# Neighbourhood attention's bias rows, rotary embedding and mask: another layout in DRAM and another place in the program

## The chip, the cores and the metric

One core of a Trainium2 chip runs the whole program: TensorE (PE, with its weight loads as PEld), VectorE (DVE), ScalarE (ACT), GpSimd (POOL), SyncE (SP) and 16 DMA engines. The metric is the device time of one execution in microseconds (us); the median of three runs is compared.

## The reference

Two blocks follow each other. The first has two layers, each made of a feed-forward part, a token mixer and a second feed-forward part; the second block has four layers and isn't touched. The change lies in the token mixer of the first block, which runs once in each of its two layers. Cut to what matters:

```python
def axial_rope(x, rows):                     # on q and k of the 256 tokens of x, 8 heads of 64
    ...
    def rot(xa, pos):
        x1, x2 = jnp.split(xa, 2, axis=-1)
        return jnp.concatenate([x1 * cos - x2 * sin, x2 * cos + x1 * sin], axis=-1)

def neighbourhood_attention(q, k, v, kc, vc, rpb, rows):   # rows = 4 grid rows of 64 tokens
    dr = row_idx - r[:, None]
    dc = np.clip(j[None, :] - j[:, None] + NA_KW - 1, 0, 2 * NA_KW - 2)
    bias = rpb[:, dr + NA_KH - 1][..., dc]
    s_loc = einsum(q, k_blk) * scale
    s_loc = jnp.where(col_valid[:, None, :], s_loc + bias, NEG_INF)
    s_ctx = einsum(q, kc) * scale
    p = softmax(concat(s_loc, s_ctx))
    return p_loc @ v_blk + p_ctx @ vc

def token_mix(hx, hc, w_in, w_out, rpb, w_pool, pool_scale, with_ctx_out):
    qx, kx, vx, ux = split(hx @ w_in)        # the context's hc @ w_in too
    qx, kx = axial_rope(qx), axial_rope(kx)
    na_x = neighbourhood_attention(...)
    pool_x = pool_mix(ux, w_pool, pool_scale)          # windowed means of u
    out_x = concat(na_x, pool_x) @ w_out
```

The bias of query column j and key column c depends on c - j and on the distance of their grid rows alone; a key outside the query's 16 columns is masked.

## The kernel before

Each engine's program is written out by one function, `walk`, which runs over the same text once for each engine and emits what `pe`, `act`, `dve`, `pool` or `sp` guard; counting semaphores tie the engines together. So the order on an engine is the order of the text, and no scheduler changes it.

**Weights.** A product streams its weight matrix in slots of 256 columns and all 1024 rows. `load` (SP) brings a slot into one of 4 buffers `w_raw`; `cut` splits it, half by half, into a high part on ACT (`w_hi`, line 422) and the rest on DVE (`w_lo`, line 425), two slots ahead of PE. PE then runs three matmuls per tile (lines 433 to 435). SP loads the next slot into a buffer when `w_lo` of its old slot is written.

**The mixer** (`mix`). After the norm, POOL waits for everything that was given out before (`border`), and then issues on its DMA queue (`side_load`, line 1079) seven tables (cosines, sines, the matrix `na_swap` that swaps the halves of a rotary pair, the matrix `na_flip`, the mask, two tables of the pooling), `w_pool`, and 16 loads of the bias: for each of 4 query rows and 4 key rows, 64 partitions by 8 heads by 64 columns. Their source is `rpb_pad` in DRAM, which holds the 15 rows of each head's table, each padded to 127 entries. The source's partition pitch is 1 entry, so that partition p gets the row of query column 63 - p: the query columns land in reverse order. `side_wait` waits until every side load issued so far has landed.

PE meanwhile runs `gemm` for q, k and u (2 slot pairs of columns each; ACT evicts them, line 708), each with 512 tokens in the first layer; in the second layer, which needs no context output, q and u have 256 tokens. Then `token_major` makes v, two slots of 4 tiles; with 4 tiles its first slot uses banks 4 to 7 and its second 0 to 3, and DVE copies the tiles out (line 745) behind the cuts of the slot two ahead. POOL runs `pool_windows`, the windowed sums of u, from u's eviction on; only `pool_products`, behind the attention, reads them.

Then two steps stand between v and the attention. First the flip: 8 matmuls of `na_flip` with 512 columns of the bias (line 1290), each turning the query columns round, and behind each on DVE an add of the mask that writes the bias back (line 1295), on two banks in turn. Next `rope_na`: for each of 8 tiles of q and k a matmul with `na_swap` (line 1187), and on DVE a product with the cosines (1189), a product of the swapped tile with the sines (1191) and their sum (1193); the matmul of a tile waits for the sum two tiles before. `border` ahead of it makes PE, ACT and DVE wait for each other. After that `attention` starts: scores on PE (988), bias add and maximum on DVE (1024, 1026), exponentials on ACT (1050), scaling on DVE (1035), transposes on PE (1004), and so on, unit by unit; its first DVE instruction is the bias add of unit 0. In the first layer a second attention, of the context's own queries, follows.

`gemm` takes a generator `between`, which it steps once after each slot pair's work; `token_major` likewise after each slot.

## Time and profile before

| | us |
|---|---|
| median of three runs | 3387.26 |
| lowest and highest of them | 3385.67, 3396.62 |
| the profiled execution's own time | 3391.18 |
| its span, first to last instruction | 3389.5 |

In the span PE is busy for 3127.4 us, DVE for 1704.7, ACT for 1378.5 and POOL for 196.9. The chain that ended last runs almost wholly on PE's products. The mean granted TensorE clock is 0.951 of full speed. The first layer's mixer stands at about 494 to 690 us of the span, the second layer's at about 1580 to 1750. The table is read so: the program is one stream of products on PE, and time is lost where PE stands idle or works on small steps that wait for DVE; two such places lie between the v product and the attention, once in each layer.

### The profile page before, as it was taken

Reading aid. Unit: us, or ns where it says so; the run is one execution under the profiler, and the core shown is the slowest. Engines: PE = TensorE matmul, PEld = TensorE weight load, DVE = VectorE, ACT = ScalarE, POOL = GpSimd, SP = SyncE. Lnnn points to the kernel's source line nnn. Section 1 sums busy time; section 2 is a strip of 40 time slices with the busy share of each in tenths; the row PEclk is TensorE's granted clock in tenths of the full one; section 3 lists DMA queues with packets and bytes.
Section 4 is the critical chain, followed back from the end, with each engine's and each line's share of the span. In section 5 each row is a group of like instructions: output and inputs, shape, how many; then the busy total and the mean of one; then the engine's idle time right before and its main releaser. Section 6 shows DMA issues by size and latency. Waiting matters only on the chain. (4 is left out here: it accounts for less than half of the span.)

```text
span 3389.5 us, 54017 instructions
## 1 busy us (share of the span) xinstructions
PE 3127.4 (92%) x21980; PEld 2738.3 (81%) x21980; DVE 1704.7 (50%) x2636; ACT 1378.5 (41%) x2238; POOL 196.9 (6%) x292
## 2 busy tenths in 40 slices
PE   6999989789999899997889989997799999988998
PEld 4877857467787688876679888997599999988998
DVE  3332262643322533226555547655576677555765
ACT  3222242432222333224255445545364546444654
POOL 1111014001111000001200000000000000000000
PEclk8999989989999899998889999998799999999999
DMA  7555334025554223343325533553155455543453
GB/s 253 174 170 164 100 112 128 1 92 163 168 174 162 87 87 99 99 137 104 87 80 194 187 124 110 193 183 120 38 163 195 156 174 174 187 149 125 150 191 107
DMA packets 403824, 471.35 MB, mean 139 GB/s; under 512 B 9660, under 2 KB 381964, under 8 KB 403626
## 3 DMA queue, kind: packets, MB, share of 16 engines
q1 hardware_dynamic: 380176, 389.05, 35.5%
q0 software_dynamic: 22592, 79.20, 7.5%
q8 instruction: 146, 2.39, 0.3%
q10 hardware_dynamic: 858, 0.29, 0.0%
q14 instruction: 52, 0.43, 0.0%
HBM read 467.33 MB, written 1.20 MB: 138 GB/s over the span
## 5 line engine op out<-in xcount | busy, mean ns | idle before, releaser
L425 DVE TENSOR_TENSOR w_lo<-w_raw,w_hi 128x1024 fp32r<-128x1024 f32 x734 | 896.8, 1227 | 1315.8 <-ACT w_hi L422 1314.8
L433 PE MATMUL bank<-a_hi,w_hi 128*128 128x256 f32 (+1 forms) x3864 | 1242.2, 321 | 69.2 <-DVE a_lo L1352 16.4
L434 PE MATMUL bank<-a_lo,w_hi 128*128 128x256 f32 (+1 forms) x3864 | 1228.6, 318 | 0.0
L435 PE MATMUL bank<-a_hi,w_lo 128*128 128x256 f32 (+1 forms) x3864 | 1226.5, 317 | 0.0
L422 ACT ACTIVATE w_hi<-w_raw 128x1024 fp32r<-128x1024 f32 x734 | 771.2, 1056 | 1012.9 <-PE bank L435 993.9
L433 PEld LDWEIGHTS bank<-a_hi,w_hi 128*128 128x128 f32 x3864 | 743.3, 192 | 147.4 <-issue 81.1
L435 PEld LDWEIGHTS bank<-a_hi,w_lo 128*128 128x128 f32 x3864 | 741.7, 192 | 50.6
L434 PEld LDWEIGHTS bank<-a_lo,w_hi 128*128 128x128 f32 x3864 | 743.3, 192 | 47.7
L433 PE MATMUL bank<-h_hi,w_hi 128*128 128x256 f32 (+1 forms) x1728 | 544.3, 315 | 0.0
L434 PE MATMUL bank<-h_lo,w_hi 128*128 128x256 f32 (+1 forms) x1728 | 539.7, 312 | 0.0
L435 PE MATMUL bank<-h_hi,w_lo 128*128 128x256 f32 (+1 forms) x1728 | 539.2, 312 | 0.0
L433 PEld LDWEIGHTS bank<-h_hi,w_hi 128*128 128x128 f32 x1728 | 326.3, 189 | 30.4 <-issue 9.0
L435 PEld LDWEIGHTS bank<-h_hi,w_lo 128*128 128x128 f32 x1728 | 324.4, 188 | 21.2
L434 PEld LDWEIGHTS bank<-h_lo,w_hi 128*128 128x128 f32 x1728 | 324.4, 188 | 20.0
L487 POOL DMA_DIRECT2D m_raw<-in_w_mod x128 | 95.9, 753 | 1222.5 <-PE bank L498 1040.5
L622 ACT ACTIVATE h_hi<-tmp_y 128x256 f32 (+3 forms) x216 | 94.9, 478 | 76.7 <-DVE tmp_y L675 76.2
L626 DVE TENSOR_TENSOR h_lo<-tmp_y,h_hi 128x256 f32 (+3 forms) x216 | 99.4, 502 | 11.1 <-ACT h_hi L622 9.5
L756 PE MATMUL bank<-tmp_g,ones 128*32 128x64 f32 (+1 forms) x1040 | 53.1, 293 | 54.0 <-ACT tmp_g L776 51.1
L1636 ACT ACTIVATE tmp_g<-bank 128x256 f32<-128x256 f32 x128 | 49.1, 383 | 127.0 <-PE bank L435 126.7
L433 PE MATMUL bank<-w_hi,a_hi 128*128 128x256 f32 (+1 forms) x288 | 82.8, 288 | 10.6 <-DVE v_g L745 10.6
L696 ACT ACTIVATE z<-bank 128x512 f32<-128x512 f32 (+1 forms) x48 | 25.3, 526 | 158.9 <-PE bank L435 158.9
L756 PEld LDWEIGHTS bank<-tmp_g,ones 128*32 128x32 f32 x1040 | 22.2, 118 | 83.1 <-ACT tmp_g L776 71.9
(289 smaller groups left out, 2447.6 us busy)
## 6 DMA issues: line engine op xcount, KB each, us to landing
w_raw<-in_mlp_w SPq DMA_DIRECT2D x128, 1024.0 KB, 5.4
w_raw<-in_w_ffn_gate_up SPq DMA_DIRECT2D x88, 1024.0 KB, 5.2
m_raw<-in_w_mod POOLq DMA_DIRECT2D x128, 512.0 KB, 4.7
w_raw<-in_w_ffn_down SPq DMA_DIRECT2D x32, 1024.0 KB, 6.2
w_raw<-in_gla_w_in SPq DMA_DIRECT2D x24, 1024.0 KB, 5.3
w_raw<-in_w_in SPq DMA_DIRECT2D x16, 1024.0 KB, 6.1
w_raw<-in_ple_w_gate SPq DMA_DIRECT2D x16, 1024.0 KB, 5.2
w_raw<-in_w_ffn_down SPq DMA_DIRECT2D x16, 768.0 KB, 6.2
```

The costliest lines, as they stand in the source:

```text
L422: e.activation(hi, raw, ACT.Copy).then_inc(S.hi_ready.sem, 1)
L425: e.tensor_tensor(lo, raw, hi.bitcast(F32), ALU.subtract).then_inc(S.lo_ready.sem, 1)
L433: e.matmul(dst, hi, rhs_hi, start=start, stop=False)
L434: e.matmul(dst, hi, rhs_lo, start=False, stop=False)
L435: return e.matmul(dst, lo, rhs_hi, start=False, stop=stop)
L487: e.dma_start(m_raw[:, half, :, :], w[:, k0:k0 + 4, ms * SC:ms * SC + SC] if i is None else w[:, k0:k0 + 4, bass.ds(e.snap(i * (per * SC) ...
L622: e.activation(hidden_at(h_hi_f, p, m, i, per, n), tmp_y[:, m, 0:n], ACT.Copy).then_inc(S.hidden_hi.sem, 1)
L626: e.tensor_tensor(hidden_at(h_lo_f, p, m, i, per, n), tmp_y[:, m, 0:n], hidden_at(h_hi_f, p, m, i, per, n).bitcast(F32), ALU.subtract).the ...
L696: e.activation(dst, b[m][:, 0:n], ACT.Copy).then_inc(S.act_evicted.sem, 1)
L756: mm = e.matmul(dst[32 * g:32 * g + 32, 0:w], ones[:, 0:32], src[:, g * w:g * w + w], start=start, stop=stop)
L1636: e.activation(tmp_g[:, m, 0:T], b[m][:, 0:T], ACT.Relu).then_inc(S.act_evicted.sem, 1)
```

## The change

Four things, in both layers.

1. **Bias rows in DRAM.** A new step `repeat_bias`, at the end of the first feed-forward part ahead of its `post_norm`, makes POOL issue 7 DMAs from DRAM to DRAM. Each writes, for one distance of grid rows, the 127 padded entries of 8 heads 64 times over into `rpb_rows`, at a pitch of 128 entries. The 16 bias loads of `mix` then read with a partition pitch of 127 entries, which steps back one entry per query column: the columns land in the right order. Number and shape of the 16 loads stay.
2. **No flip.** The table `na_flip`, its load, its 8 matmuls and 8 DVE adds are gone. The mask is added by `mask_bias`: 2 DVE instructions of 128x2048, both inputs and the output in SBUF, between the two slots of v.
3. **Rotary embedding inside u.** `rope_na` stands after the first slot pair of u's product. Its 8 matmuls go to banks 4 to 7, two to a bank, and wait for nothing of DVE; DVE waits for pairs of them. Ahead of it PE and DVE wait for all side loads (`side_wait`) and for the eviction of q and k. `token_major` now takes banks 0 to 3 for its first slot and 4 to 7 for its second; the second waits for the rotary sums (`at.roped`).
4. **The border before the attention is gone.** PE waits for the copies of v's first slot alone.

The diff, cut to its core:

```diff
@@ token_major
-                turn = 1 if tb > 2 else 0
...
-                        if s == 1:
+                        if s == 1 and tb == 2:
                             e.wait_ge(S.act_evicted.sem, last[0])
                             e.wait_ge(S.dve_evicted.sem, last[1])
+                        if s == 1 and tb > 2:
+                            e.wait_ge(S.dve.sem, at.roped)
...
                         for t in range(tb):
+                            if s == 0 and tb > 2 and t % 2 == 0:
+                                e.wait_ge(S.act_evicted.sem, last[0] - (0 if t else lag[0]))
...
@@ ffn
+                if f == 0:
+                    repeat_bias(layer)
                 post_norm(layer, 4 * f + 1, 6 * f + 2, n, 0.5)
@@
-            def rope_na():
+            def repeat_bias(layer):
+
+                if pool:
+                    side_wait()
+                per_head = 2 * NA_KH - 1
+                for d in range(2 * ROWS - 1):
+                    first = layer * NA_HEADS * per_head + NA_KH - ROWS + d
+                    side_load(rpb_rows[layer, d, :, :, 0:127],
+                              bass.AP(tensor=rpb_pad, offset=first * 127, ap=[[per_head * 127, NA_HEADS], [0, GRID_W], [1, 127]]))
+
+            def rope_na(qk_done):
 
                 base_p, base_d = S.pe.n, S.dve.n
+                if pe or dve:
+                    side_wait()
+                    e.wait_ge(S.act_evicted.sem, qk_done)
                 for j in range(8):
-                    b = bank[6 + j % 2][:, 0:T]
+                    b = bank[4 + j // 2][:, (j % 2) * T:(j % 2) * T + T]
                     if pe:
-                        if j >= 2:
-                            e.wait_ge(S.dve.sem, base_d + 3 * (j - 1))
                         e.matmul(b, Z["na_swap"][:, :], qk[:, j, 0:T], start=True, stop=True).then_inc(S.pe.sem, 1)
...
+            def mask_bias():
+
+                if dve:
+                    side_wait()
+                    for q in range(2):
+                        rows = bias[:, q, :, :].rearrange("p h (r c) -> p (h r) c", c=GRID_W)
+                        e.tensor_tensor(rows, rows, Z["na_mask"][:, :].unsqueeze(1).to_broadcast([P, NA_HEADS * ROWS, GRID_W]),
+                                        ALU.add).then_inc(S.dve.sem, 1)
...
@@ mix
-                            src = bass.AP(tensor=rpb_pad, offset=(layer * rpb_rows + NA_KH - 1 + kr - qrow) * 127,
-                                          ap=[[1, GRID_W], [(2 * NA_KH - 1) * 127, NA_HEADS], [1, GRID_W]])
+                            first = (layer * (2 * ROWS - 1) + ROWS - 1 + kr - qrow) * NA_HEADS * GRID_W * P + GRID_W - 1
+                            src = bass.AP(tensor=rpb_rows, offset=first,
+                                          ap=[[P - 1, GRID_W], [GRID_W * P, NA_HEADS], [1, GRID_W]])
...
                 gemm(w, [(0, DK)], 2, 2, a_op(n), copy_to(ut[:].rearrange("p a t -> p (a t)"), TT, n), S.act_evicted,
-                     first_col=3 * NA_WIDTH)
+                     first_col=3 * NA_WIDTH, between=rope_na(qk_done))
                 pool_windows(n)
                 fetch_table(ACT.Exp)
-                token_major(w, 2 * NA_WIDTH, 2, TT, lambda t, s: v_na[:, t, s * SC:(s + 1) * SC])
...
-                        e.matmul(b[:, :], Z["na_flip"][:, :], flat[:, c], start=True, stop=True).then_inc(S.pe.sem, 1)
...
-                if not pool:
-                    border(but=S.pool)
-                rope_na()
-                pe_wait_all()
+                values_out = S.dve_evicted.n
+                token_major(w, 2 * NA_WIDTH, 2, TT, lambda t, s: v_na[:, t, s * SC:(s + 1) * SC], mask_bias())
+
+                if pe:
+                    e.wait_ge(S.dve_evicted.sem, values_out + 4)
```

Three places in the new order. First DVE in the first layer's mixer, from the cuts of the q, k and u products to the attention (each row: line, instruction, tiles and size; xN is a run of N). Before:

```order
L425 TENSOR_TENSOR w_lo<-w_raw,w_hi 128x8x128 x14
L745 COPY v_na<-bank 128x256 x4
L425 TENSOR_TENSOR w_lo<-w_raw,w_hi 128x8x128 x2
L745 COPY v_na<-bank 128x256 x4
L1295 TENSOR_TENSOR bias<-bank,na_mask_s 128x512 x8
L1189 TENSOR_TENSOR tmp_g<-qk,na_cos_s 128x256
L1191 TENSOR_TENSOR tmp_y<-bank,na_sin_s 128x256
L1193 TENSOR_TENSOR qk<-tmp_g,tmp_y 128x256
...
L1024 TENSOR_TENSOR bank<-bank,bias 128x2x256
```

After (the lines have moved: 423 is 425 before, 1203 to 1207 are 1189 to 1193, 746 is 745, 1027 is 1024):

```order
L423 TENSOR_TENSOR w_lo<-w_raw,w_hi 128x8x128 x10
L1203 TENSOR_TENSOR tmp_g<-qk,na_cos_s 128x256
L1205 TENSOR_TENSOR tmp_y<-bank,na_sin_s 128x256
L1207 TENSOR_TENSOR qk<-tmp_g,tmp_y 128x256
...
L423 TENSOR_TENSOR w_lo<-w_raw,w_hi 128x8x128 x4
L746 COPY v_na<-bank 128x256 x4
L1219 TENSOR_TENSOR bias<-bias,na_mask_s 128x2048 x2
L423 TENSOR_TENSOR w_lo<-w_raw,w_hi 128x8x128 x2
L746 COPY v_na<-bank 128x256 x4
L1027 TENSOR_TENSOR bank<-bank,bias 128x2x256
```

The 24 rotary instructions (eight times the three rows) moved ahead of four cuts and of v's copies, the mask's eight adds became two between v's slots, and the last copies of v stand right ahead of the first bias add.

Second PE in the same layer. Before, behind the last matmul of v:

```order
L435 MATMUL bank<-w_hi,a_lo 128x256
L1290 MATMUL bank<-bias,na_flip_s 128x512 x8
L1187 MATMUL bank<-qk,na_swap_s 128x256 x8
L988 MATMUL bank<-qk 128x512 x6
L1004 MATMUL bank<-eye,prob 128x128 x8
```

After, in the middle of u's product (431 to 433 are the lines of the products):

```order
L432 MATMUL bank<-a_lo,w_hi 128x512
L433 MATMUL bank<-a_hi,w_lo 128x512
L1201 MATMUL bank<-qk,na_swap_s 128x256 x8
L431 MATMUL bank<-a_hi,w_hi 128x512
L432 MATMUL bank<-a_lo,w_hi 128x512
```

The flip is gone, the eight swaps stand between u's first and second slot pair, and the scores follow v's last matmul.

Third POOL's queue from the first layer's last loads of modulation weights (`m_raw`) to the pooling. After (before, the second row wasn't there, `na_flip_s` was loaded behind `na_swap_s`, and the bias came from `rpb_pad`):

```order
L485 DMA m_raw<-in_w_mod 128x4x256 x24
L1082 DMA rpb_rows<-rpb_pad 512x1x127 x7
L1082 DMA na_cos_s<-table_na_cos 128x256
L1082 DMA na_sin_s<-table_na_sin 128x256
L1082 DMA na_swap_s<-table_na_swap 128x128
...
L1082 DMA w_pool_s<-in_w_pool 128x4x128
L1082 DMA bias<-rpb_rows 64x8x64 x16
L1242 MEMSET pool_a 128x320
```

Seven DMAs came in ahead of the tables, and one table left the queue. The second layer has the same three changes.

## Rows read from the trace of the kernel before

**Rows 1.** The table of stretches, first layer: stretch, its length, busy times, PEclk, DMA.

```profile
core 0: us, PE busy (x) PEld busy (x) DVE busy (x) ACT busy (x) POOL busy (x), PEclk, DMA share, GB/s
582.30:588.10 5.80, 0.00 (x0) 0.01 (x1) 4.50 (x6) 2.00 (x2) 5.34 (x7) 0.75 0.04 8
588.10:598.40 10.30, 9.48 (x16) 3.28 (x16) 5.53 (x8) 0.00 (x0) 9.17 (x16) 0.81 0.30 99
598.40:608.10 9.70, 5.30 (x16) 2.46 (x16) 9.39 (x24) 0.00 (x0) 0.71 (x1) 1.00 0.00 0
```

**Rows 2.** The same table, second layer: behind the v product, flip.

```profile
1651.00:1655.90 4.90, 0.00 (x0) 0.00 (x0) 3.69 (x6) 2.00 (x2) 0.00 (x0) 0.77 0.04 9
1655.90:1666.40 10.50, 9.68 (x16) 3.36 (x16) 5.51 (x8) 0.00 (x0) 0.00 (x0) 0.78 0.29 97
```

**Rows 3.** Instructions in order of time, first layer: start, us, engine, line, [idle before <-releaser].

```profile
583.47 3.17 DVE L425 TENSOR_TENSOR w_lo<-w_raw,w_hi 128x1024 fp32r<-128x1024 f32 x2 [7.33 <-ACT w_hi L422]
586.57 1.41 DVE L745 COPY v_na<-bank 128x256 f32<-128x256 f32 x4
...
609.35 0.70 DVE L1024 TENSOR_TENSOR bank<-bank,bias 128x512 f32<-128x512 f32 x1 [1.25 <-PE bank L988]
```

**Rows 4.** The same view, DVE, second layer.

```profile
1652.17 2.36 DVE L425 TENSOR_TENSOR w_lo<-w_raw,w_hi 128x1024 fp32r<-128x1024 f32 x2 [7.28 <-ACT w_hi L422]
1654.45 1.41 DVE L745 COPY v_na<-bank 128x256 f32<-128x256 f32 x4
1678.20 0.70 DVE L1024 TENSOR_TENSOR bank<-bank,bias 128x512 f32<-128x512 f32 x1 [2.18 <-PE bank L988]
```

**Rows 5.** The same view, PE, first layer: the rotary swaps, two records to a matmul.

```profile
598.43 1.10 PE L1187 MATMUL bank<-qk,na_swap_s 128*128 128x256 f32 x4 [0.83 <-issue]
600.24 0.70 PE L1187 MATMUL bank<-qk,na_swap_s 128*128 128x256 f32 x2 [0.71 <-DVE qk L1193]
```

**Rows 6.** The same view, POOL: issues of the bias loads in both layers.

```profile
506.81 2.76 POOL L1079 DMA_DIRECT2D bias<-rpb_pad  x4
...
529.35 3.39 POOL L1079 DMA_DIRECT2D bias<-rpb_pad  x5 [6.96 <-issue]
...
1593.87 2.76 POOL L1079 DMA_DIRECT2D bias<-rpb_pad  x4
...
1617.57 3.39 POOL L1079 DMA_DIRECT2D bias<-rpb_pad  x5 [7.42 <-issue]
```

**Rows 7.** The bias tile: landing times of the last five (first layer), last two (second).

```profile
DMA to landing us min/median/max: 4.9/7.1/7.2
...
DMA to landing us min/median/max: 7.1/7.3/7.5
```

**Rows 8.** Instructions in order of time, ACT: last eviction of u's first pair, both layers.

```profile
548.41 0.60 ACT L708 ACTIVATE ut<-bank 128x512 f32<-128x512 f32 x1 [3.89 <-PE bank L435]
...
1622.23 0.38 ACT L708 ACTIVATE ut<-bank 128x256 f32<-128x256 f32 x1 [1.55 <-PE bank L435]
```

**Rows 9.** The same view, DVE, first layer, during the u and v products.

```profile
549.99 1.23 DVE L425 TENSOR_TENSOR w_lo<-w_raw,w_hi 128x1024 fp32r<-128x1024 f32 x1 [4.21 <-ACT w_hi L422]
555.43 1.23 DVE L425 TENSOR_TENSOR w_lo<-w_raw,w_hi 128x1024 fp32r<-128x1024 f32 x1 [4.21 <-ACT w_hi L422]
...
574.74 1.40 DVE L745 COPY v_na<-bank 128x256 f32<-128x256 f32 x4
```

**Rows 10.** The qk tile, all its cosine products: min/median/max ns.

```profile
L1189 DVE TENSOR_TENSOR tmp_g<-qk,na_cos_s x16: 417/419/969, 598.4 to 1674.8; 128x256 f32<-128x256 f32 x16
```

**Rows 11.** Instructions in order of time, POOL: a pooling step, and the idle time before the tables.

```profile
502.33 0.55 POOL L1079 DMA_DIRECT2D na_cos_s<-table_na_cos  x1 [55.31 <-issue]
...
598.39 0.73 POOL L1225 TENSOR_TENSOR ut<-pool_b,ut 128x256 f32<-128x256 f32 x1
...
1589.40 0.55 POOL L1079 DMA_DIRECT2D na_cos_s<-table_na_cos  x1 [94.42 <-ACT qk L708]
```

**Rows 12.** DMA queue of POOL, stretch 506 to 560: packets, MB, share of 16 engines.

```profile
q0 software_dynamic: 1050, 3.02, 25.4%
```

More of the change, by code:

```diff
@@ L169, in constants @@
     c["na_cos"], c["na_sin"], c["na_swap"] = cos, sin, swap
-    eye_row = np.eye(GRID_W, dtype=np.float32)[::-1]
-    c["na_flip"] = np.kron(np.eye(P // GRID_W, dtype=np.float32), eye_row)
     col = np.arange(GRID_W)
@@ L270, in build @@
             Z["na_swap"] = sb("na_swap_s", [P, P], F32, h)
-            Z["na_flip"] = sb("na_flip_s", [P, P], F32, h)
             Z["na_mask"] = sb("na_mask_s", [P, GRID_W], F32, h)
@@ L333, in build @@
         rpb_pad = nc.dram_tensor("rpb_pad", [DEPTH, NA_HEADS * (2 * NA_KH - 1), 127], F32)
+        rpb_rows = nc.dram_tensor("rpb_rows", [DEPTH, 2 * ROWS - 1, NA_HEADS, GRID_W, P], F32)
         total, shift_from = [], []
@@ L738, in token_major @@
                                 v_hi, v_lo = (cut_slot(x, nn)[:, k, :] for x in (w_hi, w_lo))
-                                mm = three(bank[(s + turn) % 2 * tb + t][:, 0:SC], x_hi, x_lo, v_hi, v_lo, k == 0, k == DK - 1)
+                                mm = three(bank[s % 2 * tb + t][:, 0:SC], x_hi, x_lo, v_hi, v_lo, k == 0, k == DK - 1)
                         mm.then_inc(S.slot_used.sem, 2)
@@ L744, in token_major @@
                         for t in range(tb):
-                            e.tensor_copy(dst(t, s), bank[(s + turn) % 2 * tb + t][:, 0:SC]).then_inc(S.dve_evicted.sem, 1)
+                            e.tensor_copy(dst(t, s), bank[s % 2 * tb + t][:, 0:SC]).then_inc(S.dve_evicted.sem, 1)
                     S.dve_evicted.n += tb
@@ L1189, in rope_na @@
                         e.tensor_tensor(tmp_g[:, j % 2, 0:T], qk[:, j, 0:T], Z["na_cos"][:, :], ALU.mult).then_inc(S.dve.sem, 1)
-                        e.wait_ge(S.pe.sem, base_p + j + 1)
+                        e.wait_ge(S.pe.sem, base_p + 2 * (j // 2) + 2)
                         e.tensor_tensor(tmp_y[:, j % 2, 0:T], b, Z["na_sin"][:, :], ALU.mult).then_inc(S.dve.sem, 1)
@@ L1195, in rope_na @@
                 S.dve.n += 24
+                at.roped = S.dve.n
+                yield
+            def mask_bias():
[5 more added lines that the diff above has]
+                                        ALU.add).then_inc(S.dve.sem, 1)
+                S.dve.n += 2
+                yield
             def pool_windows(n):
@@ L1256, in mix @@
                     border()
-                for name in ("na_cos", "na_sin", "na_swap", "na_flip", "na_mask", "pool_row", "pool_ctx"):
+                for name in ("na_cos", "na_sin", "na_swap", "na_mask", "pool_row", "pool_ctx"):
                     side_load(Z[name][:], C[name][:])
                 side_load(Z["w_pool"][:, :, :], A["w_pool"][layer].rearrange("g c d -> c g d"))
-                rpb_rows = NA_HEADS * (2 * NA_KH - 1)
                 for qt in range(2):
@@ L1273, in mix @@
                 gemm(w, [(0, DK)], 2, 2, a_op(TT), copy_to(qk_f[:, 4 * TT:], TT, TT), S.act_evicted, first_col=NA_WIDTH)
+                qk_done = S.act_evicted.n
                 gemm(w, [(0, DK)], 2, 2, a_op(n), copy_to(ut[:].rearrange("p a t -> p (a t)"), TT, n), S.act_evicted,
-                     first_col=3 * NA_WIDTH)
+                     first_col=3 * NA_WIDTH, between=rope_na(qk_done))
                 pool_windows(n)
                 fetch_table(ACT.Exp)
-                token_major(w, 2 * NA_WIDTH, 2, TT, lambda t, s: v_na[:, t, s * SC:(s + 1) * SC])
-                flat = bias[:, :, :, :].rearrange("p q h c -> p (q h c)")
-                base_p, base_d = S.pe.n, S.dve.n
-                for j in range(8):
-                    c, b = slice(j * 512, j * 512 + 512), bank[4 + j % 2]
-                    if pe:
-                        if j == 0:
-                            side_wait()
-                            e.wait_ge(S.dve_evicted.sem, S.dve_evicted.n)
-                        if j >= 2:
-                            e.wait_ge(S.dve.sem, base_d + j - 1)
-                        e.matmul(b[:, :], Z["na_flip"][:, :], flat[:, c], start=True, stop=True).then_inc(S.pe.sem, 1)
-                    if dve:
-                        if j == 0:
-                            side_wait()
-                        e.wait_ge(S.pe.sem, base_p + j + 1)
-                        e.tensor_tensor(flat[:, c].rearrange("p (r c) -> p r c", c=GRID_W), b[:, :].rearrange("p (r c) -> p r c", c=GRID_W),
-                                        Z["na_mask"][:, :].unsqueeze(1).to_broadcast([P, 512 // GRID_W, GRID_W]), ALU.add).then_inc(S.dve.sem, 1)
-                S.pe.n += 8
-                S.dve.n += 8
-                if not pool:
-                    border(but=S.pool)
-                rope_na()
-                pe_wait_all()
+                values_out = S.dve_evicted.n
+                token_major(w, 2 * NA_WIDTH, 2, TT, lambda t, s: v_na[:, t, s * SC:(s + 1) * SC], mask_bias())
+                if pe:
+                    e.wait_ge(S.dve_evicted.sem, values_out + 4)
+                if dve:
+                    e.wait_ge(S.dve.sem, S.dve.n)
                 def head_rows(m):
```

## The prediction, made before the changed kernel ran

> **What bounds the kernel now.** I read the table of stretches first, since the change touches two places only, the way from the v product to the attention in each layer. PE's v product ends at 582.3 in the first layer and at 1651.0 in the second. Behind it PE does nothing for 5.8 and 4.9 us, then works at flips for 10.3 and 10.5 us, and in the first layer at the rotary step for 9.7 us, in which DVE is busy for 9.39 us [rows 1, 2]. Next the rows in order of time. What the attention starts with on DVE is its first bias add, at 609.35 and 1678.20 [rows 3, 4]. From there it runs the same units as before, so I take the gain of a layer as the time by which this instruction comes earlier. In each place a chain decides, not an engine's load: DVE's cuts and copies of v, then flips and mask adds in turn, then 24 rotary instructions. Without flip and rotary step, what is late next is DVE, which has two cuts and four copies to do after v: it is free at 586.57 + 1.41 = 587.98 and at 1654.45 + 1.41 = 1655.86 [rows 3, 4].
>
> **What goes.** From DVE's last copy to the bias add: 609.35 - 587.98 = 21.4 us and 1678.20 - 1655.86 = 22.3 us, **43.7 us** in all. Flips, mask adds, rotary step, border and the first score's way (1.25 us and 2.18 us of waiting, rows 3 and 4) all lie in it. The scores of units 0 and 1 now run on PE beside DVE's cuts and copies, since PE waits only for the copies of v's first slot, and their banks (0 to 3) are the ones these copies empty.
>
> **What the swaps cost on PE.** Eight matmuls now stand in the midst of u's product, where PE is fully busy. Two took 1.10 us and one alone 0.70 [rows 5], so each further one adds 0.40: 0.70 + 7 x 0.40 = **3.5 us** a layer, 7.0 in all; at 1.10 a pair it would be 4.4 a layer. Everything behind them is later by that. They wait for nothing of DVE, since each has a half bank of its own.
>
> **What the rotary instructions cost on DVE.** 24 instructions, some 9.7 us [rows 1], go between the cuts. In the first layer the cut ahead of them ends at 549.99 + 1.23 = 551.2, so they end near 561; the cut that stood at 555.43, then due near 558.9, slips to 561 [rows 9]. It feeds v's second slot. DVE copied v's first slot from 574.74 on, behind two cuts [rows 9], so PE wants the second near 571 + 3.5, 13 us later: nothing. The next load of weights slips with it, under a stock of four buffers: nothing. PE's new wait for the last rotary sum stands ahead of that same slot: nothing. If this cover were gone, the cost would be the 2 us by which the cut slips.
>
> **The mask.** Two instructions of 2048 columns, both inputs in SBUF. A cut of 1024 columns takes 1.23 us [rows 9], a product of 256 takes 0.42 [rows 10]: 1.055 ns a column, so 2.3 us each, 4.6 in all. POOL's windows run beside them. What that does, the cuts show: two took 3.17 us where POOL was at work and 1.23 each where it wasn't [rows 1, 3, 9], and one cosine product took 969 ns instead of 419 while POOL's step of 0.73 us began at 598.39 [rows 10, 11]. So up to 6.1 us. They start at 574.74 + 1.40 + 3.5 = 579.6 in the first layer [rows 9] and end by 585.7 at the latest; the next work on DVE comes at 583.47 + 3.5 = 587.0 [rows 3]. Hidden, with 1.3 us to spare at worst.
>
> The Trainium skill says of this (SBUF — State Buffer, Who interferes with whom) that a VectorE instruction with two SBUF inputs shares a read port with GpSimd instructions that read SBUF, one of them blocking the other whole. By that rule the 0.55 us of the cosine product is a full block, and these rows agree.
>
> What isn't hidden: the first layer's attention now starts while POOL's windows still run. They end near 599.1 [rows 11]; with the later u and the mask in their way near 604, and DVE's attention starts at 591.5. Three or four units, each with two scalings in SBUF, could wait up to 0.5 us apiece, 3.5 us at most, nothing at least; I take **1.5 us**. In the second layer the windows end before the attention.
>
> **The new wait for the side loads.** PE and DVE now wait, after u's first slot pair, until all 16 bias loads have landed; before, this wait came after v and never ended last. Queued behind it are PE's swaps, u's second pair and all of v. First layer: the last load's issue ends at 529.35 + 3.39 = 532.7, one issue is 0.69, so it begins at 532.1, and lands 7.2 us later at 539.3 [rows 6, 7]. PE arrives as ACT evicts u's first pair, at 548.4 [rows 8]: nothing, with 9 us to spare. Second layer: q and u have half the tokens, and PE arrives at **1622.2** [rows 8]. The last load begins at 1617.57 + 3.39 - 0.69 = 1620.3 and lands 7.1 to 7.5 us later, at 1627.4 to 1627.8 [rows 6, 7]; without the load of the flip table, one issue of about 0.54 [rows 11], at **1627.1**. So a stall of **5 us**, the one new wait on the path. If POOL's bursts of issues fell otherwise it could be 0 or 8.
>
> A stall brings the clock down: behind the idle 5.8 and 4.9 us the flips had a granted clock of 0.81 and 0.78 [rows 1, 2], which between the levels of 2.4 and 1.2 GHz is 0.38 x 10.3 = 3.9 and 0.44 x 10.5 = 4.6 us at half speed. Half of that is lost: **2 us**. DVE's mask and rotary work come later with PE and stay covered; the cuts of the second half of u come after the rotary sums.
>
> **Repeating the rows.** Seven DMAs a layer of 512 rows of 508 bytes, 260 KB each. They stand in POOL's queue behind the last loads of modulation weights, and ahead of a stretch in which POOL has nothing to do for 55 and 94 us [rows 11]. Issued like the bias loads (a burst, a pause of some 8 us, another), they need about 15 us, and land within 10 more. What they move, 1.8 MB, costs by the rate of POOL's queue: 0.254 x 16 x 54 us over 1050 packets is 0.21 us for 2.9 KB [rows 12], so 1.8 MB is about 8 us of all 16 engines. PE's weights are four slots ahead. Cost nothing; if that cover were gone, up to 8 us a layer. The Trainium skill speaks against this step (DMA: Bandwidth & Descriptors, Specifications): below 512 bytes the transfer isn't at line rate and turns into a read-modify-write. No row here shows a write of 508 bytes; even at three times the price the step would end within POOL's idle time, so the sum stays.
>
> **The sum.** 43.7 gone; 7.0 for swaps, 5 for the stall, 2 for the clock and 1.5 for POOL's windows added: a gain of **28.2 us**. The first layer gives 21.4 - 3.5 - 1.5 = 16.4, the second 22.3 - 3.5 - 7 = 11.8. The profiled execution's own time of 3391.18 would become 3363.0. It lies 3.9 us above the median of the runs, which is what counts: 3387.26 - 28.2 = **3359**.
>
> **The rivals.**
> *No stall in the second layer.* If the loads from the new rows land 5 us sooner, the 7 us of stall and clock stay: gain 35, 3352. For it: three bursts at some 12 us each leave room for one burst fewer, with one table less in the queue [rows 6]. Against it: the number of loads is the same.
> *The bias loads get slower, and it ends slower than before.* A load's 512 pieces of 256 bytes used to come from a few KB that overlap; now they come from 8 blocks 32 KB apart at a pitch of 508 bytes. From first issue to last landing it takes 539.3 - 506.8 = 32.5 us and 1627.6 - 1593.9 = 33.7 us now [rows 6, 7]. Stretched by f, it stalls PE by 32.5 f - 42 in the first layer and by 33.7 f - 29 in the second. Without stalls the change gains 43.7 - 7.0 - 1.5 = 35 us, so it breaks even, with the clock, at f = 1.55. At f = 2 the stalls are 23 and 38 us, with the clock 65: slower by 30, 3417. For it: the wait moved ahead of v, 29 us after the first issue. Against it: pieces, bytes and issues are the same, and the pauses between bursts are POOL's. At f from 1.2 to 1.5 the gain shrinks to between 19 and 4 us.
> *The start isn't what counts.* Could the attention be held by PE or ACT instead of DVE, or the product behind it start no sooner? POOL's windows, near 604, are far from the pooling's products, which stand behind the attention. Then only half would come through: 14 us, 3373. I see no row for it.
>
> **How the numbers follow.** Forecast (28 us, give or take 6) 0.62; no stall 0.14; loads slower by 1.2 to 1.5, or half of it lost, 0.14, of which 0.04 is a gain too small to tell; a stretch near break-even 0.04; slower 0.06. About 0.3%, 10 us, can be told from no change. So faster 0.86, same 0.08, slower 0.06. The range is 3350 to 3374: it takes in the case without a stall, swaps at 4.4, a stall of 8, and a partly stretched load; beyond it lie about 2 in 10.
>
> **What would show it.** In the changed profile: no flip; swaps of 3.5 us between u's pairs in both layers; ahead of them in the second layer a PE idle time of about 5 us ended by a side load, none in the first; two mask instructions of 2.3 to 3 us between v's copies; DVE's first bias add right behind v's last copy, 5 to 6 us after v's end; the repeats on POOL well before the norm's end. It is wrong if the side loads land late in the first layer too, if the mask pushes v's cuts, or if PE stops at the end of the first feed-forward part, where the repeats move data.

## The result, and the profile after

The changed kernel takes **3357.09 us** (median of 4 runs, 3344.98 to 3360.89), the kernel before 3391.85 in 4 runs (3385.67 to 3396.62): a ratio of 0.9892, with a 95% interval of 0.9877 to 0.9907. The profiled execution took 3360.89 us, with a span of 3358.5. Forecast were 3359 us and a gain of 28.2 us; between the medians the gain is **34.8 us**. The number was met more closely than the gain, since the kernel before has a median 4.6 us higher over 4 runs than over the 3 runs that the forecast started from.

The first layer, DVE in order of time (start, us, engine, line, what, idle time before and what ended it):

```profile
550.05 1.22 DVE L423 TENSOR_TENSOR w_lo<-w_raw,w_hi 128x1024 fp32r<-128x1024 f32 x1 [4.21 <-ACT w_hi L420]
551.19 0.42 DVE L1203 TENSOR_TENSOR tmp_g<-qk,na_cos_s 128x256 f32<-128x256 f32 x1
...
559.88 0.43 DVE L1207 TENSOR_TENSOR qk<-tmp_g,tmp_y 128x256 f32<-128x256 f32 x1
560.23 1.22 DVE L423 TENSOR_TENSOR w_lo<-w_raw,w_hi 128x1024 fp32r<-128x1024 f32 x1
...
578.29 1.40 DVE L746 COPY v_na<-bank 128x256 f32<-128x256 f32 x4
579.62 5.03 DVE L1219 TENSOR_TENSOR bias<-bias,na_mask_s 128x2048 f32<-128x2048 f32 x2
587.03 2.94 DVE L423 TENSOR_TENSOR w_lo<-w_raw,w_hi 128x1024 fp32r<-128x1024 f32 x2 [2.39 <-ACT w_hi L420]
589.90 1.40 DVE L746 COPY v_na<-bank 128x256 f32<-128x256 f32 x4
591.23 0.68 DVE L1027 TENSOR_TENSOR bank<-bank,bias 128x512 f32<-128x512 f32 x1
```

The rotary step is done by 560.3, within u's product; the mask stands between v's first copies and its last cuts; and the first bias add follows the last copy with no gap, where [rows 3] had 21.4 us between them. The same in the second layer, to be held against [rows 4]:

```profile
1631.64 5.42 DVE L1219 TENSOR_TENSOR bias<-bias,na_mask_s 128x2048 f32<-128x2048 f32 x2
1638.47 2.89 DVE L423 TENSOR_TENSOR w_lo<-w_raw,w_hi 128x1024 fp32r<-128x1024 f32 x2 [1.41 <-ACT w_hi L420]
1641.29 1.40 DVE L746 COPY v_na<-bank 128x256 f32<-128x256 f32 x4
1642.61 0.68 DVE L1027 TENSOR_TENSOR bank<-bank,bias 128x512 f32<-128x512 f32 x1
```

The same view for ACT, the last eviction of u's first pair, in both layers; then for PE, the swaps at the same places.

```profile
548.48 0.60 ACT L706 ACTIVATE ut<-bank 128x512 f32<-128x512 f32 x1 [3.90 <-PE bank L433]
...
1605.08 0.38 ACT L706 ACTIVATE ut<-bank 128x256 f32<-128x256 f32 x1 [1.55 <-PE bank L433]
```

```profile
548.28 3.62 PE L1201 MATMUL bank<-qk,na_swap_s 128*128 128x256 f32 x16
...
1604.88 3.62 PE L1201 MATMUL bank<-qk,na_swap_s 128*128 128x256 f32 x16
```

Neither row of swaps has idle time before it. The stall forecast for the second layer isn't there. With this eviction as zero, the first bias add stood at 60.94 us before (609.35 - 548.41) and stands at 42.75 now (591.23 - 548.48): 18.2 us gained in the first layer. In the second, 1678.20 - 1622.23 = 55.97 has become 1642.61 - 1605.08 = 37.53: **18.4 us**, where 11.8 were forecast. Together that is 36.6 us. The second layer's first bias add comes 35.6 us earlier; the 1.0 us between lies behind the first layer's first bias add, from which to the second layer's eviction of u it takes 1013.9 us instead of 1012.9.

Why PE didn't wait shows on POOL, where the seven repeats come first and then, in both layers, the issues of the side loads:

```profile
447.05 1.67 POOL L1082 DMA_DIRECT2D rpb_rows<-rpb_pad  x2
450.14 0.79 POOL L1082 DMA_DIRECT2D rpb_rows<-rpb_pad  x1 [1.41 <-issue]
457.58 2.36 POOL L1082 DMA_DIRECT2D rpb_rows<-rpb_pad  x3 [6.66 <-issue]
467.31 0.79 POOL L1082 DMA_DIRECT2D rpb_rows<-rpb_pad  x1 [7.37 <-issue]
502.49 0.58 POOL L1082 DMA_DIRECT2D na_cos_s<-table_na_cos  x1 [34.39 <-issue]
...
506.46 2.10 POOL L1082 DMA_DIRECT2D bias<-rpb_rows  x3
512.99 4.79 POOL L1082 DMA_DIRECT2D bias<-rpb_rows  x7 [4.43 <-issue]
522.19 4.11 POOL L1082 DMA_DIRECT2D bias<-rpb_rows  x6 [4.41 <-issue]
...
1576.28 2.07 POOL L1082 DMA_DIRECT2D bias<-rpb_rows  x3
1586.50 4.83 POOL L1082 DMA_DIRECT2D bias<-rpb_rows  x7 [8.15 <-issue]
1594.85 4.08 POOL L1082 DMA_DIRECT2D bias<-rpb_rows  x6 [3.52 <-issue]
```

Before, the bursts were 4, 7 and 5 loads with pauses of 8.07 and 6.96 us in the first layer and 8.76 and 7.42 in the second. Now they are 3, 7 and 6, with pauses of 4.43 and 4.41, and of 8.15 and 3.52. From the first issue to the end of the last, the loads take 19.8 and 22.7 us, not 25.9 and 27.1 [rows 6], and in the second layer the last lands 3.4 us after its issue instead of 7.1 to 7.5 [rows 7]. That is at 1598.2 + 3.4 = 1601.6, and PE comes at 1604.88.

### The profile page after: what moved, and what is told of

Read it like the earlier page. It is cut to its first block and busy times, and to the rows that moved or that the text cites. A ratio compares the mean times of both kernels' runs of the same rounds, so it can differ in the third digit from the quotient of the medians.

```text
span 3358.5 us, 53925 instructions
## 1 busy us (share of the span) xinstructions
PE 3108.9 (93%) x21948; PEld 2741.9 (82%) x21948; DVE 1706.7 (51%) x2624; ACT 1377.6 (41%) x2238; POOL 216.4 (6%) x304
```

## The experiments

Executions of one kernel scatter by 10 to 20 us, so a difference of a few us is read from the trace, at three places. The last two columns are the program's unchanged rest: from that bias add to the start of the second block (POOL's load of `in_p`), and from there to the end of the span.

| kernel | first bias add, layer 1 | layer 2 | to the second block | to the end |
|---|---|---|---|---|
| before | 609.35 | 1678.20 | 276.0 | 1435.3 |
| after | 591.23 | 1642.61 | 280.4 | 1435.5 |
| after, again | 590.35 | 1641.30 | 282.9 | 1433.9 |
| old source | 589.78 | 1640.67 | 277.6 | 1435.9 |
| rotary step alone | 600.66 | 1670.81 | 279.4 | 1440.4 |
| no flip alone | 604.59 | 1664.88 | 282.5 | 1440.8 |
| no repeats | 591.88 | 1648.73 | 278.5 | 1421.6 |
| table back | 591.65 | 1648.61 | 278.2 | 1433.6 |
| repeats twice | 591.99 | 1644.88 | 278.7 | 1422.8 |
| late cuts | 586.37 | 1634.45 | 277.7 | 1435.2 |
| late cuts, again | 586.92 | 1635.16 | 277.4 | 1440.4 |
| loads made twice | 603.74 | 1683.32 | 285.5 | 1428.8 |
| no windows | 588.89 | 1639.87 | 278.0 | 1436.9 |
| neither flip nor windows | 599.42 | 1657.66 | 277.5 | 1433.6 |

### Does the source set the pace of the loads?

Theory A: reading from the repeated rows makes a load land sooner. Theory B: the new source isn't the cause. The changed kernel, with the loads pointed at the old rows at the old pitch:

```diff
-src = bass.AP(tensor=rpb_rows, offset=first, ap=[[P - 1, GRID_W], [GRID_W * P, NA_HEADS], [1, GRID_W]])
+src = bass.AP(tensor=rpb_pad, offset=(layer * NA_HEADS * (2 * NA_KH - 1) + NA_KH - 1 + kr - qrow) * 127,
+              ap=[[1, GRID_W], [(2 * NA_KH - 1) * 127, NA_HEADS], [1, GRID_W]])
```

> The changed kernel, but its 16 bias loads read the padded table at the old pitch of one entry again (so the bias rows reach the attention with the query columns reversed); the repeats are still made. Question: why did the bias loads take some 25 us instead of 33, so that no stall came in the second layer? Theory A, the source sets the pace (64 partitions reading overlapping bytes are slow): the loads take 32 to 34 us again in both layers, PE waits about 5 us for a side load after u's first pair in the second layer, the time is 5 to 7 us above the changed kernel's (about 3363 against 3357). Theory B, the queue does it (one table fewer, other bursts): the loads stay at 23 to 25 us, no stall, same time as the changed kernel.

Measured: 3357.25 us (4 runs, 3354.30 to 3365.02), a ratio to before of 0.9899 (0.988 to 0.9918). The bursts are 3, 7 and 6 loads, the last landing in the second layer is at about 1600.5, and there is no stall. Theory A falls: where the bytes come from doesn't matter. The rival by which the new pitch slows the loads falls with it.

### The rotary step alone

The kernel before, with the eight swaps and 24 rotary instructions inside u's product; flip and mask adds stay behind v:

```diff
-     first_col=3 * NA_WIDTH)
+     first_col=3 * NA_WIDTH, between=rope_na(qk_done))
...
-rope_na()
```

> The kernel before with only the rotary step moved into u's product (with the banks of v turned round as in the change); flips, mask adds and old bias source stay. Theory: the rotary step's 9.7 and 10 us leave the way to the attention, 3.5 us of swaps a layer come in, and with the old source the second layer stalls 5 us with 2 us of clock: a gain of about 6 us, 3386 against 3392. Rival, no stall even with the old source: a gain of about 13 us, 3379.

Measured: 3391.75 us against 3394.96, a ratio of 0.9993 (0.9979 to 1.0008; 10 runs): nothing that can be told from no change, and too little for the rival's 13 us. In the first layer the bias add is 54.4 us from u's eviction instead of 60.9, a gain of 6.5; in the second it is 58.9 instead of 56.0, a loss of 3.0. There the bursts are 4, 7 and 5 as before, and the stall that the prediction had foreseen appears. PE in order of time:

```profile
1618.49 6.00 PE L1191 MATMUL bank<-qk,na_swap_s 128*128 128x256 f32 x16 [6.65 <-DMA bias<-rpb_pad]
```

The list of waits from 1605 to 1630 (who waited for what: us in all, times, longest):

```profile
PE bank L1191 <- DMA bias<-rpb_pad: 6.7, 1, 6.7
```

The swaps take 6.00 us behind the stall and 3.62 without one: 2.4 us of clock, where the prediction had put 2. So the mechanism exists and was sized nearly right (6.7 and 2.4 against 5 and 2); it is the changed kernel that doesn't meet it.

### The flip gone alone

The changed kernel, with the rotary step back behind v, and its border:

```diff
-     first_col=3 * NA_WIDTH, between=rope_na(qk_done))
+     first_col=3 * NA_WIDTH)
...
+if not pool:
+    border(but=S.pool)
+next(rope_na(qk_done))
+pe_wait_all()
```

> The changed kernel with the rotary step back behind v, with the border ahead of it: only the flip goes, and the mask moves between v's slots. Theory: the flips' 10.3 and 10.5 us go, nothing comes in: a gain of 19 to 22 us against the kernel before, about 3371. Rival, that the border and v's copies hide a part: a gain under 15 us.

Measured: 3380.34 us (5 runs, 3377.68 to 3390.44), a ratio of 0.9958 (0.9944 to 0.9972): 14 us gained, not 21. The table of stretches, from the end of v's last copy to the first bias add, in both layers (stretch, length, busy time and count of PE, PEld, DVE, ACT and POOL, PEclk, DMA share, GB/s):

```profile
587.30:604.60 17.30, 7.71 (x22) 5.44 (x24) 13.19 (x25) 0.00 (x0) 14.11 (x22) 0.70 0.17 59
1651.70:1664.90 13.20, 7.78 (x22) 5.43 (x24) 8.97 (x26) 0.00 (x0) 0.00 (x0) 0.76 0.23 77
```

DVE in order of time, in the first of them:

```profile
590.57 0.94 DVE L1201 TENSOR_TENSOR tmp_g<-qk,na_cos_s 128x256 f32<-128x256 f32 x1
591.44 0.41 DVE L1203 TENSOR_TENSOR tmp_y<-bank,na_sin_s 128x256 f32<-128x256 f32 x1
```

In the first layer the step takes 17.3 us and DVE is busy for 13.2 of them: POOL's windows, which the flips used to cover, now run beside it, and most products with the cosines, whose two inputs lie in SBUF, take 0.85 to 0.96 us instead of 0.42. The product with a bank as input keeps 0.41. In both layers the clock is low, which it had not been behind the flips of the first [rows 1]. The gain lies on the rival's side of 15 us, but not for the rival's reason: ahead of the first rotary instruction, where the border stands, DVE idles for 0.4 us only. That is also all that any run shows of the border's price; none took it away alone.

The same kernel without POOL's windows:

```diff
-pool_windows(n)
```

> The kernel without the flip and with the rotary step still behind v, now also without the pooling's windows. With the windows the rotary step of the first layer took from 587.3 to the bias add at 604.6, 17.3 us, where before the flips it had taken 11.4. Theory, two causes: the windows block the cosine and sum instructions on DVE (about 4 us of the 6), and the swaps start at a low clock since nothing warms PE ahead of them (about 2 us). Without the windows it takes 13 to 13.5 us, as in the second layer. Rival, the clock alone: it stays at 17 us.

Measured: 3370.39 us in one run, and 13.2 us from v's last copy to the bias add in the first layer, against 17.3. So the windows cost 4.1 us there. What is left stands 2.2 us in the first layer and 1.4 in the second above rotary step and first score of before (609.35 - 598.4 = 11.0 and 1678.2 - 1666.4 = 11.8). In both layers of this run the granted clock of the stage is 0.76, and the eight swaps take about 5.8 us where they take 3.62 inside u's product. That the clock is the cause of the rest is likely, but no run separates it from the new order of waits.

By the medians the parts alone give 3 us (not told from nothing) and 14 us, the whole gives 35. By the bias add's distance from u's eviction it is 6.5 - 3.0 = 3.5 us for the rotary step, 4.3 + 9.0 = 13.3 us for the flip, and 36.6 us for the whole. Each part alone leaves work behind v, and puts it where something else costs it: the rotary step moved alone meets the loads, the flip gone alone uncovers windows and clock.

### Why the loads come sooner

Now the question was what makes the bursts differ. Theory C: the repeats ahead in the queue; theory D: the table that is gone. Without the repeats, and with the old source of the loads, which the first experiment shows to change nothing:

```diff
-if f == 0:
-    repeat_bias(layer)
```

> The changed kernel with the old source of the bias loads and without the 14 repeats (the bias rows arrive with the query columns reversed). Question: what made the bias loads quick, since the old source kept them quick. Theory C, the repeats, which stand in POOL's queue ahead of them, leave the queue in another state, so that the bursts of issues fall as 3, 7 and 6: without them the bursts are 4, 7 and 5 or the like again, the loads take 30 to 34 us, PE waits 5 to 7 us for a side load in the second layer, and the time is 7 to 9 us above the changed kernel's (3364 to 3366). Theory D, the missing flip table does it: bursts 3, 7, 6, 23 to 26 us, no stall, 3357.

Measured: 3354.46 us (4 runs, 3350.45 to 3359.58), a ratio of 0.9887 (0.987 to 0.9903). POOL in order of time, second layer, and PE's swaps:

```profile
1576.45 3.43 POOL L1080 DMA_DIRECT2D bias<-rpb_pad  x5
1588.48 4.75 POOL L1080 DMA_DIRECT2D bias<-rpb_pad  x7 [8.60 <-issue]
1600.43 2.72 POOL L1080 DMA_DIRECT2D bias<-rpb_pad  x4 [7.19 <-issue]
...
1609.59 5.41 PE L1199 MATMUL bank<-qk,na_swap_s 128*128 128x256 f32 x16 [4.30 <-DMA bias<-rpb_pad]
```

The stall of 4.3 us is there, and the bias add stands 43.40 us behind u's eviction instead of 37.53. So 5.9 us up to the second layer's attention hang on the repeats being in the queue. The total time doesn't show them: 7 to 9 us above the changed kernel were expected, and the median lies 2.6 below it. In the profiled execution the second block, which the edit doesn't touch, was 14 us faster (the table above); the other three executions have no trace. So whether the 5.9 us reach the end isn't shown.

With the flip's table loaded again, unused:

```diff
-for name in ("na_cos", "na_sin", "na_swap", "na_mask", "pool_row", "pool_ctx"):
+for name in ("na_cos", "na_sin", "na_swap", "na_flip", "na_mask", "pool_row", "pool_ctx"):
```

> The changed kernel with the flip table loaded again, though nothing reads it: an eighth load ahead of the bias loads. Theory C (the repeats decide): the bias loads stay at 23 to 26 us and PE doesn't wait in the second layer. Theory D (the table decides): 32 to 34 us, and a stall of 5 to 7 us there.

Measured: 3362.07 us (one run), with bursts of 2, 7 and 7. Both theories fail. It is fast in the first layer and not in the second, where these rows stand on POOL and PE:

```profile
1587.23 4.76 POOL L1085 DMA_DIRECT2D bias<-rpb_rows  x7 [8.98 <-issue]
1598.50 4.75 POOL L1085 DMA_DIRECT2D bias<-rpb_rows  x7 [6.51 <-issue]
...
1609.47 5.41 PE L1204 MATMUL bank<-qk,na_swap_s 128*128 128x256 f32 x16 [4.41 <-DMA bias<-rpb_rows]
```

With the repeats issued twice:

```diff
-for d in range(2 * ROWS - 1):
+for d in [*range(2 * ROWS - 1)] * 2:
```

> The changed kernel with every repeat made twice, 14 DMAs a layer in place of 7. Theory that their own time is hidden in POOL's idle stretch: the norm behind them starts no later, and PE idles no longer at the end of the first feed-forward part. By theory C the bursts of the bias loads shift once more: first burst other than 3, span of the loads anything from 23 to 34 us; by theory D they stay at 3, 7, 6.

Measured: 3348.01 us (one run), with bursts of 1, 7, 7 and 1, and a stall of 1.57 us in the second layer. The tables' first issue comes at 503.21 instead of 502.49, and at 503.09 without any repeat: 14 repeats still cost the norm nothing. In the second layer the same: from the first layer's bias add to the eviction of u it takes 1013.5 us with 14 repeats and with none.

Neither C nor D alone, then, but **when a burst meets a weight load**. Two rules hold for the side loads in all these traces. The first burst, tables included, is 12 loads without repeats (8 + 4, or 7 + 5), 10 with seven repeats (7 + 3, or 8 + 2) and 8 with fourteen (7 + 1); each later one is 7 or the rest. (The repeats themselves go out three at a time at most.) And a pause ends about 0.4 us after the whole burst ahead of it has landed. Most bias loads land 3 to 5 us after their issue, or 6 to 9 where one of SP's loads of 1 MB is issued during the burst. The second burst of the second layer, beside the issue of SP's weight load next to it:

| kernel | second burst | SP's weight load | longest landing | pause behind | stall |
|---|---|---|---|---|---|
| before | 1605.39 to 1610.16 | 1608.43 | 7.7 | 7.42 | the wait stood behind v |
| rotary step alone | 1596.53 to 1601.31 | 1598.08 | 7.9 | 7.57 | 6.65 |
| old source | 1584.53 to 1589.38 | 1589.34 | 4.2 | 3.85 | 0 |
| repeats twice | 1585.33 to 1590.09 | 1591.69 | 4.0 | 3.63 | 1.57 |
| after | 1586.50 to 1591.33 | 1591.28 | 3.8 | 3.52 | 0 |
| table back | 1587.23 to 1591.99 | 1591.31 | 6.8 | 6.51 | 4.41 |
| no repeats | 1588.48 to 1593.23 | 1591.53 | 7.5 | 7.19 | 4.30 |

The landing times of this burst in the changed kernel, and then in the kernel without repeats:

```profile
DMA to landing us min/median/max: 3.1/3.6/3.8
```

```profile
DMA to landing us min/median/max: 3.0/3.3/7.5
```

The changed kernel's burst ends as the weight load is issued, and with the table back, where it ends 0.7 us later, the pause is 3 us longer. The first layer agrees: before, the second burst stood from 517.64 to 522.39 about a weight load issued at 518.61, and its longest landing was 7.3 us; in the changed kernel it ended at 517.78, ahead of the load at 518.66, and its longest was 4.7. No run moved the weight load alone, so this is read from the traces and not shown by an edit. The stall of "repeats twice" has another cause: its sixteenth load needs a fourth burst. The Trainium skill (DMA: Bandwidth & Descriptors, Queues, rings and completion order) says that each DMA engine takes the queues for which it has work in turn, a packet at a time; the longer landings beside a weight load (7.5 against 3.8 us) agree with it, but no run here shows the turns themselves. What in the queue sets the length of the first burst wasn't tried and stays open.

### Is the new wait on the path at all?

Each bias load issued twice, the second time into a buffer that isn't in use then:

```diff
 side_load(bias[half * GRID_W:(half + 1) * GRID_W, qt, :, kr * GRID_W:(kr + 1) * GRID_W], src)
+other = (prob, probT)[qt][half * GRID_W:(half + 1) * GRID_W, :, :, :].rearrange("p a b (c d) -> p (a b c) d", d=T)
+side_load(other[:, :, kr * GRID_W:(kr + 1) * GRID_W], src)
```

> The changed kernel with each bias load made a second time, into buffers that are free then: 32 loads. It prices the new wait. Theory: the side loads take about 48 us, so PE waits after u's first pair about 4 to 8 us in the first layer and about 20 us in the second, both ended by a side load, and the time is 25 to 35 us above the changed kernel's, near that of the kernel before. Rival, that PE's wait is covered by other slack: under 10 us.

Measured: 3399.3 us (one run), 42 above the changed kernel and 5 above the kernel before. PE's swaps of the first layer:

```profile
558.90 5.47 PE L1201 MATMUL bank<-qk,na_swap_s 128*128 128x256 f32 x16 [9.27 <-DMA probT<-rpb_rows]
```

And of the second:

```profile
1643.90 5.69 PE L1201 MATMUL bank<-qk,na_swap_s 128*128 128x256 f32 x16 [24.30 <-DMA probT<-rpb_rows]
```

Both stalls, 9.3 and 24.3 us, are longer than expected, and so is the loss (42 us, expected 25 to 35). The first bias add of the second layer is 40.7 us later than in the changed kernel. So the wait is on the path in both layers, and the loads' pace decides on which side of zero it falls: the mechanism of the rival that ended slower is real, and only its cause, the pitch, isn't.

### The price of POOL's windows

The changed kernel without them (the rotary step stays where the change puts it):

```diff
-pool_windows(n)
```

> The changed kernel without the pooling's windows on POOL (u goes into the pooling's products as it is). It prices what POOL's windows cost DVE in the first layer. Theory, the shared port: the two mask instructions take 2.3 us each in place of 2.5 to 2.8, the four scalings of the units that ran beside the windows take 0.88 a pair in place of 1.2 to 1.55, and the eighth bias add of the first layer comes 23 us after the first instead of 23.8; 1 to 2 us in all in this stage, too little for the total time to show. Rival, that the slower scalings were covered by waits anyway: the distance from the first to the eighth bias add stays.

Measured: 3357.08 us (one run). A step of the windows beside the mask in the changed kernel, POOL in order of time:

```profile
579.66 2.84 POOL L1252 TENSOR_TENSOR ut<-pool_b,ut 128x256 f32<-128x256 f32 x1
```

The mask and a pair of scalings without the windows, DVE in order of time:

```profile
577.38 4.48 DVE L1219 TENSOR_TENSOR bias<-bias,na_mask_s 128x2048 f32<-128x2048 f32 x2
...
592.81 0.88 DVE L1038 TENSOR_SCALAR prob<-prob,stat 128x512 f32<-128x512 f32 x2
```

The mask takes 4.48 us without the windows and 5.03 beside them, and POOL's step beside it 2.84 instead of 0.73. From first to eighth bias add it is 23.2 us instead of 23.8: the windows cost the attention 0.6 us, with scalings of 1.2 to 1.6 us a pair instead of 0.88. Another 0.6 us lies ahead of it: the first bias add stands 42.16 us behind u's eviction instead of 42.75, since v's last two cuts take 2.36 us instead of 2.94. The kernel before paid that too (3.17 us, [rows 3]). By the Trainium skill (SBUF — State Buffer, Who interferes with whom) the one that comes second is blocked whole; the step on POOL, longer by 2.1 us where one mask instruction takes 2.3, agrees.

### One step further

Now v's last cuts, which serve the output product, stand ahead of the attention on DVE. Made behind `pool_products` instead:

```diff
-ahead(nn, None, 0)
+if s < slots - 1 or tb == 2:
+    ahead(nn, None, 0)
...
 pool_products(layer, n)
+ahead(at.slot - 1, None, 0)
```

> The changed kernel with one more move: the cuts of the second slot of the output product, which stand ahead of v's last copies on DVE, are made after the pooling's products instead. Theory that DVE's work behind v is what the attention waits for: DVE is free 1.4 us after v instead of 5 to 6, then the first score (about 2.9 us after v's end) ends last, so the first bias add comes 2 to 3 us earlier in each layer and the time is about 5 us below the changed kernel's (3352). Rival, that the late cuts are then waited for by the output product, or that POOL's windows hold the attention back: no gain, or 2 to 4 us lost.

Measured: 3355.44 us (4 runs), a ratio of 0.9898 (0.9878 to 0.9918). In the trace, DVE copies v and adds the bias at once:

```profile
585.04 1.42 DVE L747 COPY v_na<-bank 128x256 f32<-128x256 f32 x4 [1.24 <-PE bank L433]
586.37 0.69 DVE L1028 TENSOR_TENSOR bank<-bank,bias 128x512 f32<-128x512 f32 x1
```

To tell, both kernels were run again on one chip.

> The changed kernel with the two cuts behind v made after the pooling's products. In its first profile the first bias add came 3.9 us earlier behind u's eviction in the first layer and 4.0 in the second. Theory, that this is on the path: 3 to 8 us below the changed kernel. Rival, that the late cuts or POOL's windows take it back: no difference.

> The changed kernel once more, beside the next one on the same chip: 1.0 to 1.2 per cent below the kernel before.

Measured: 3353.97 us with late cuts (6 runs, 3340.42 to 3363.89; ratio 0.9886, 0.9867 to 0.9905), and 3359.08 for the changed kernel (5 runs, 3349.82 to 3361.14; ratio 0.9899, 0.9884 to 0.9914). By the trace the bias add comes about 4 us sooner in each layer (38.74 and 33.58 us behind u's eviction, not 42.75 and 37.53), and the second layer's stands at 1634.45 and 1635.16 against 1640.67 to 1642.61. About 1 us of this is lost again on the way to the second layer (1014.5 and 1014.7 us from the first bias add to u's eviction, against 1013.9 and 1013.4). Over both sets of runs the medians are 3354.8 and 3359.1. By the trace the attention starts sooner; between the medians the 4 us aren't told apart from scatter, as the intervals overlap.

## Why the prediction was right, and where it wasn't

The time was met within 2 us and the gain missed by 6.6, and that the first is so close is luck: the 7 us of stall and clock that didn't come were made up for by a start value, 3387.26, that lay 4.6 us below the median over 4 runs. Term by term:

- **What goes, 43.7 us**: right. DVE was what came last, and the bias add follows its last copy with no gap in either layer. From the same eviction on, the first layer gains 18.2 (21.4 - 3.5 = 17.9 worked out), the second 18.4 (22.3 - 3.5 = 18.8).
- **Swaps**: 3.62 us a layer, forecast 3.5. They wait for nothing of DVE.
- **Rotary instructions**: 9.1 us from 551.19 on, forecast 9.7; the slipped cut at 560.23, forecast 561; nothing waits for it.
- **Mask**: 5.03 and 5.42 us, inside the forecast 4.6 to 6.1, and hidden: DVE still idles 2.39 and 1.41 us before v's next cuts.
- **POOL's windows**: 0.6 us, forecast 1.5. They run until 606.9 and not 604; single steps of theirs take up to 2.84 us beside the mask and the cuts.
- **Repeats**: 20 us from first issue to last, forecast 15, and landings of 6.1 to 8.5 in the first layer; the norm's end is where it was (502.49 against 502.33). The Trainium skill's rule against writes below 512 bytes (DMA: Bandwidth & Descriptors, Specifications) wasn't put to the test, as no run repeated rows of 512 bytes; what the runs show is that the repeats, once or twice over, delay nothing that is on the path.
- **The new wait for the side loads, 5 us and 2 for the clock: this step failed.** It took the pace of the loads (three bursts, pauses of 7 and 8 us, landing after 7.1 to 7.5) unchanged from the trace of before, corrected only by one table's issue. The changed kernel's own queue has another rhythm: the repeats shorten the first burst by two loads, and with the flip's table gone as well the second burst ends at 1591.33, just as SP's weight load is issued (1591.28), so that the last load lands 3.3 us before PE comes. Either alone isn't enough: without the repeats PE stalls for 4.30 us, with the table back for 4.41. The rival "no stall" gave the gain as 35 us, but neither of its reasons is what happened: the new rows aren't what makes the loads land sooner, and there are still three bursts. Nearer was the remark that bursts falling otherwise could make the stall 0 or 8.
- **The clock**: no stall, no loss. Where stalls were made, it cost 1.8 to 2.4 us on the swaps, as forecast.
- **The loads get slower**: no; neither pitch nor source matters. Two figures of this rival don't follow from its own formula: at f of 1.2 and 1.5 it leaves a gain of about 22 and 3 us, not 19 and 4. Nothing rests on them.
- **The start isn't what counts**: no. The first bias add of the second layer is 35.6 us earlier. The profiled span is shorter by 31.0 only; the 4.6 lie behind that bias add, in work that is unchanged, and the table of kernels shows that stretch between 276.0 and 285.5 us, with the kernel before at the low end. What goes with it is the granted clock (the third number from the right), here in two stretches of the changed kernel behind the attention:

```profile
1676.00:1724.40 48.40, 36.89 (x326) 32.57 (x325) 23.62 (x45) 22.29 (x42) 0.00 (x0) 0.76 0.27 88
1724.40:1764.40 40.00, 40.00 (x337) 40.00 (x337) 22.93 (x33) 20.55 (x30) 0.00 (x0) 0.95 0.46 150
```

The answering stretches of before have 0.82 and 1.00. Whether this is chance of the execution, or something of the changed kernel, one trace of before can't tell; it stays open.

## What to carry to other kernels

Work between a product and the step that it feeds can move inside the product, if it needs nothing of it. There it costs only its time on the engine that is busy (3.6 us of swaps a layer here), and nothing on those that have room. But take everything out of the gap at once, since each part alone left another obstacle in it (3.5 and 13.3 us alone, 36.6 together). When a wait is moved ahead, its price hangs on the rhythm of a queue that the same change alters: give the stall a range that reaches to nothing, and look what else is in that queue. And read an edit of a few us at a fixed place in the trace, not from the total, where unchanged code scatters by more.

## What the hardware did that I had not expected

- POOL's queue issues bias loads in bursts of seven, and goes on about 0.4 us after the whole burst has landed; 7 or 14 transfers issued long before shorten the burst behind them by 2 or 4 loads.
- One weight load of 1 MB that meets a burst raises its longest landing from 3.8 to 7.5 us and so moves all later bursts; 0.7 us between two kernels' bursts decided whether they met.
- With the flips taken away, the rotary stage behind v had a granted clock of 0.70 to 0.76; behind the flips it had 1.00 in the first layer [rows 1].
